# The forget gate of a two-block transformer kernel: logits with tokens on partitions instead of heads on partitions

## The chip, the cores and the metric

The kernel is one program on one core of a Trainium2 chip. The metric is the device time of one execution in microseconds. The kernel before the change takes 981.37 us (median of three runs, 980.94 to 981.79).

## The reference, cut to what matters

Two transformer blocks run on 256 tokens of width 1024 in float32. The first has a mixer (a gated convolution beside "forgetting attention" with eight heads) and a SwiGLU layer; the second has two SwiGLU layers, a hybrid mixer and an attention over a memory. The change touches the forget gate of the first block alone:

```python
f_logit = (h @ w_in)[..., 1536:1544]          # eight heads, 1024 inputs
logf = log_sigmoid(f_logit + b_f)             # [256 tokens, 8 heads]
c = cumsum(logf, axis=tokens)
logits = q @ k.T / 8 + c[query] - c[key]      # per head, then the causal mask and the softmax
```

Here h is x after its RMS norm. The kernel multiplies by the gain ahead of the product and by the inverse deviation of the token behind it.

## The kernel before, in words

**Tiling.** Activations stand transposed, features on partitions and the 256 tokens along the row, as eight tiles of 128 x 256 (act_hi, act_lo). To get float32 accuracy from fp32r matmuls, each weight and each activation is split in a high and a low part, and a product is three matmuls (`three`, L426 to L430): high by high, high by low, low by high. All weights come as 161 chunks of 1 MB through a ring of three stages. SyncE issues a chunk's DMA when VectorE has freed its place; ScalarE copies it to w_hi (`hi`), VectorE subtracts to w_lo (`lo`), and TensorE multiplies (`up`, `up_tok`, `down`). The order on each engine is written out by hand, and engines meet only at semaphores.

**The forget gate.** It lies in the first mixer, between the chunks of q and k (0 to 3) and those of v (4, 5), g_b (6, 7) and g_c (8, 9):

- SyncE loads the eight columns of w_in to wf (L381), and four copies of b_f into row 102 of par_rows, at columns 0, 32, 64 and 96 (L313).
- ScalarE and VectorE write wf four times over, 32 columns apart, into zeroed tiles wf_hi and wf_lo of 8 x 128 columns (L1128, L1694). GpSimd zeroes them at the start (L2131, L2132).
- TensorE transposes the parameter rows (L680) and then multiplies (L683): for each of eight k, `three` with the 128 columns of wf_hi or wf_lo stationary and 256 tokens moving, so 24 matmuls. The result stands in bank AUX with 128 partitions (four copies of eight heads, the rest zero) and 256 tokens along the row.
- VectorE scales by rs, adds the bias and forms -|z| (L1710 to L1713), ScalarE takes exp and ln (L1136, L1138), VectorE subtracts (L1717). All are 128 x 256 wide.
- TensorE turns the logarithm by two transposes (L695) after chunk 7, VectorE copies it to logf_tok (L1728), TensorE goes through chunk 8 and then sums it with the triangular matrix tri (L699 to L703), which gives c with tokens on partitions (c_tok, L1733) and with heads on partitions (negc, L1149). `aux` makes TensorE wait for the bank AUX. A_F, A_LOGF and A_CUM number its uses.

The names of the tiles: gate_banks in a row of the trace is the bank AUX in this stretch (it is the fourth half of that tensor), up_banks holds the results of `up`, mix_hi and mix_lo hold wf_hi and wf_lo, forget holds fz, fe and logf.

Of the kernel before, what the change touches and what calls it, by code (L numbers as in the profile page):

```python
# [14 lines left out]
F32 = mybir.dt.float32  # L15
F32R = mybir.dt.float32r
ALU = mybir.AluOpType
ACT = mybir.ActivationFunctionType
AX = mybir.AxisListType.X

P = 128
T = 256
D = 1024
KD = D // P
# [8 lines left out]
Q, K, V, GB, GC, HC, GATE_C, GATE_A = 0, 2, 4, 6, 8, 10, 12, 16  # L33
# [42 lines left out]
N_X0, N_MEM, N_POST0, N_FFN0, N_POST1, N_FFN1, N_MIX2, N_MEMQ, N_FFN2, N_OUT = range(10)  # L76
ROWS = [N_X0, N_FFN0, N_FFN1, N_MIX2, N_FFN2]


A_F, A_LOGF, A_CUM = 0, 1, 2  # L80
A_DQ = [3, 4]
A_DK = [5, 6]
A_BEFORE_FFN = [3, 3, 7]


G_MIX_PRE, G_MIX_POST, G_FFN_PRE, G_FFN_POST = 0, 8, 16, 24
G_FFN1, G_MIX2, G_MEMQ, G_MEMKV, G_FFN2 = 32, 40, 48, 56, 64
CONV, RETN, DIFN, MQN, MKN, DQN, DKN, LAMQ, LAMK, BF = 80, 92, 93, 94, 96, 98, 99, 100, 101, 102

C_ID, C_ONE, C_HALVES, C_TRI, C_CAUSAL, C_END = 0, 128, 256, 384, 640, 896  # L90

# [1 line left out]
def build(nc, a, out):  # L93
    with ExitStack() as ctx:
# [11 lines left out]
        act_hi, act_lo = act_both[:, :, 0, :], act_both[:, :, 1, :]  # L106
        mix_hi = sb("mix_hi", [P, KD, T], F32R)
        mix_lo = sb("mix_lo", [P, KD, T], F32R)
# [6 lines left out]
        rs = sb("rs", [P, T])  # L115
# [14 lines left out]
        par = sb("par", [P, P])  # L130
        first_rows = sb("first_rows", [KD, P])
        first_gain = sb("first_gain", [P, KD])
        wf = sb("wf", [P, KD, 8])
        forget = sb("forget", [P, 4, T])
        fz, fe, logf = (forget[:, i, :] for i in range(3))
        logf_tok = sb("logf_tok", [P, 2, P])
        c_tok = sb("c_tok", [P, 2, 8])
        small = sb("small", [P, 160])
# [7 lines left out]
        mem_T = q_pad[:, :, :, :].rearrange("p a b t -> p (a b) t")  # L146
        p_T0 = mem_T
        p_T1 = k_T[:, :, :].rearrange("p a b -> p (a b)").rearrange("p (m q) -> p m q", m=8)
        wf_hi = mix_hi[:, 0:4, :].rearrange("p a b -> p (a b)").rearrange("p (k n) -> p k n", k=KD)
        wf_lo = mix_lo[:, 0:4, :].rearrange("p a b -> p (a b)").rearrange("p (k n) -> p k n", k=KD)  # L150
        v_flat = v_mem[:, :, :].rearrange("p a b -> p (a b)")
        gb_T = v_flat[:, 0:1024].rearrange("p (a t) -> p a t", a=4)
        hc_T = v_flat[:, 1024:2048].rearrange("p (j a t) -> p j a t", j=2, a=2)
# [7 lines left out]
        sel_r = mix_hi[:, 4:8, :].rearrange("p a b -> p (a b)").rearrange("p (h m) -> p h m", h=8)  # L161
        negc = mix_lo[:, 4, :]
        q_T = q_pad[:, 0, :, :]
        wf_hi4, wf_lo4 = (w.rearrange("p k (g n) -> p k g n", g=4)[:, :, :, 0:8] for w in (wf_hi, wf_lo))
        wf4 = wf[:, :, None, :].to_broadcast([P, KD, 4, 8])
        alibi, decay = table[:, 0:4, :], table[:, 4:8, :]
        k_sq = [gate[:, 4 + 2 * t:6 + 2 * t, :].rearrange("p a b -> p (a b)") for t in range(2)]
        raw_dq = [gate[:, 8 + 2 * t:10 + 2 * t, :].rearrange("p a b -> p (a b)") for t in range(2)]
# [13 lines left out]
        ident = const[:, C_ID:C_ID + P]  # L182
# [7 lines left out]
        mean_sq, deviations, factors = ([norms[:, at + 2 * n:at + 2 * n + 2] for n in range(10)] for at in (40, 60, 80))  # L190
# [12 lines left out]
        bank = [x[:, i, :] for x in (up_banks, gate_banks) for i in range(2)]  # L203
# [3 lines left out]
        UP, SUM, AUX, ACC = 0, 2, 3, 4  # L207
# [84 lines left out]
        def parameters(engine):  # L292

            engine.wait_ge(zeroed, 3)

            def rows(r, n, src, cols=P, at=0):
                engine.dma_start(par_rows[r:r + n, at:at + cols], src).then_inc(par_landed, 16)

            for r, name in ((G_MIX_PRE, "norm_mix_pre"), (G_FFN_PRE, "norm_ffn_pre"), (G_FFN1, "norm_ffn1_2"), (G_MIX2, "norm_mix_2"),
                            (G_MEMQ, "norm_mem_q_2"), (G_MEMKV, "norm_mem_kv_2"), (G_FFN2, "norm_ffn2_2")):  # L300
                rows(r, KD, a[name][0].rearrange("(k p) -> k p", p=P))
            rows(CONV, 12, a["conv_w"][0].rearrange("j (b p) -> (j b) p", p=P))
            rows(RETN, 1, a["ret_norm_2"])
            rows(DIFN, 1, a["diff_norm_2"])
            rows(MQN, 2, a["mem_q_norm_2"][0].rearrange("(k p) -> k p", p=P))
            rows(MKN, 2, a["mem_k_norm_2"][0].rearrange("(k p) -> k p", p=P))
            for r, name in ((DQN, "diff_q_norm_2"), (DKN, "diff_k_norm_2")):
                rows(r, 1, a[name], 64, 0)
                rows(r, 1, a[name], 64, 64)
            for r, at, name in ((LAMQ, 0, "lambda_q1_2"), (LAMQ, 64, "lambda_q2_2"),  # L310
                                (LAMK, 0, "lambda_k1_2"), (LAMK, 64, "lambda_k2_2")):
                rows(r, 1, a[name], 64, at)
            for at in range(0, P, 32):  # L313
                rows(BF, 1, a["b_f"], 8, at)

        def store(engine, t, j):
            cols = slice(512 * j, 512 * j + 512)
# [107 lines left out]
        def _(pe):  # L425
            def three(dst, w, lo_w, x, lo_x, first, last, group=True):  # L426

                pe.matmul(dst, w, x, start=first, stop=False, skip_group_check=not group)  # L428
                pe.matmul(dst, w, lo_x, start=False, stop=False, skip_group_check=not group)  # L429
                return pe.matmul(dst, lo_w, x, start=False, stop=last, skip_group_check=not group)  # L430
# [38 lines left out]
            def up(c, hi, lo, ready=None, base=0, between=None):  # L469
                up_bank(c)  # L470
                up_product(pair[UP + BANK[c]], c % RING, hi, lo, ready, base, between=between)
# [46 lines left out]
            def aux(n):  # L518
                if n:
                    pe.wait_ge(aux_free, n)  # L520
# [154 lines left out]
            up(K, act_hi, act_lo)  # L675

            up(K + 1, act_hi, act_lo)
            pe.wait_ge(par_landed, 16 * 24)
            pe.wait_ge(rs_done, 1)
            pe.transpose(bank[SUM][:, 0:P], par_rows[:, :], ident).then_inc(par_turned, 1)  # L680
            pe.wait_ge(wf_lo_done, 1)
            aux(A_F)
            for k in range(KD):  # L683
                mm = three(bank[AUX][:, 0:T], wf_hi[:, k, :], wf_lo[:, k, :], act_hi[:, k, :], act_lo[:, k, :],
                           k == 0, k == KD - 1)
            mm.then_inc(aux_done, 1)
            tokens(V, act_hi, act_lo)
            pe.wait_ge(par_ready, 2)
            pe.matmul(bank[SUM][:, 0:2], ones, lam_p, start=True, stop=True).then_inc(lam_done, 1)
            up(GB, act_hi, act_lo)  # L690
            up(GB + 1, act_hi, act_lo)
            pe.wait_ge(logf_done, 1)
            aux(A_LOGF)
            for t in range(2):
                mm = pe.transpose(bank[AUX][:, t * P:t * P + P], logf[:, t * P:t * P + P], ident)  # L695
            mm.then_inc(aux_done, 1)
            up(GC, act_hi, act_lo)
            aux(A_CUM)
            pe.matmul(bank[AUX][:, 0:8], tri[:, 0:P], logf_tok[:, 0, 0:8], start=True, stop=True)  # L699
            pe.matmul(bank[AUX][:, 8:16], tri[:, P:T], logf_tok[:, 0, 0:8], start=True, stop=False)  # L700
# [73 lines left out]
            for j in range(4):  # L774
                pe.wait_ge(act_lo_done, 8 + 2 * j + 2)
                s = slice(2 * j, 2 * j + 2)
# [218 lines left out]
        def _(act):  # L995
# [128 lines left out]
            rows_out(N_X0, SUM)  # L1124
            hi(3)
            act.wait_ge(wf_landed, 16)
            act.wait_ge(zeroed, 6)
            act.activation(wf_hi4, wf4, copy).then_inc(wf_hi_done, 1)  # L1128
            hi(4)
            hi(5)  # L1130
            hi(6)
# [365 lines left out]
        def _(dve):  # L1497
            steps = [0]

            def then(ins):  # L1500

                steps[0] += 1
                ins.then_inc(dve_step, 1)
                dve.wait_ge(dve_step, steps[0])
# [182 lines left out]
                dve.scalar_tensor_tensor(q_T[:, b:b + 2, :], src, 0.125, over(rs), ALU.mult, ALU.mult).then_inc(up_free, 1)  # L1687

            query(Q)
            dve.wait_ge(zeroed, 6)  # L1690
            lo(3)
            query(Q + 1)
            dve.wait_ge(wf_hi_done, 1)
            dve.tensor_tensor(wf_lo4, wf4, wf_hi4.bitcast(F32), ALU.subtract).then_inc(wf_lo_done, 1)  # L1694

            lo(4)
            scaled(K, k_T[:, 0:2, :], rs)
# [9 lines left out]
            lo(6)  # L1707

            dve.wait_ge(aux_done, A_F + 1)
            dve.tensor_tensor(fz, bank[AUX][:, 0:T], rs[:, :], ALU.mult).then_inc(aux_free, 1)  # L1710
            dve.wait_ge(aux_free, A_F + 1)
            then(dve.tensor_scalar(fz, fz, par[:, BF:BF + 1], None, ALU.add))
            dve.scalar_tensor_tensor(fe, fz, -1.0, fz, ALU.mult, ALU.min).then_inc(fz_done, 1)  # L1713
            lo(7)
            lo(8)
            dve.wait_ge(fln_done, 1)
            dve.scalar_tensor_tensor(logf, fz, 0.0, fe, ALU.min, ALU.subtract).then_inc(logf_done, 1)  # L1717
            scaled(GB, gb_T[:, 0:2, :], rs)
            lo(9)
            scaled(GB + 1, gb_T[:, 2:4, :], rs)  # L1720
# [3 lines left out]

            then(dve.tensor_scalar(par[:, DIFN:DIFN + 1], par[:, DIFN:DIFN + 1], 1.0 - LAM_INIT, None, ALU.mult))
            lo(10)
            dve.wait_ge(aux_done, A_LOGF + 1)
            dve.tensor_copy(logf_tok[:, :, :].rearrange("p t q -> p (t q)"), bank[AUX][:, 0:2 * P]).then_inc(aux_free, 1)  # L1728
            scaled(GC, z_T[:, 0:2, 2:T + 2], rs)
            lo(11)  # L1730
            dve.wait_ge(aux_done, A_CUM + 1)
# [387 lines left out]
        @block.gpsimd  # L2119
        def _(pool):  # L2120
            steps = [0]

            def then(ins):
                steps[0] += 1
                ins.then_inc(pool_step, 1)
                pool.wait_ge(pool_step, steps[0])

            pool.memset(small[:, :], 0.0).then_inc(zeroed, 1)
            pool.memset(eps_t[:, :], EPS).then_inc(zeroed, 1)
            pool.memset(par_rows[:, :], 0.0).then_inc(zeroed, 1)  # L2130
            pool.memset(wf_hi.bitcast(F32), 0.0).then_inc(zeroed, 1)  # L2131
            pool.memset(wf_lo.bitcast(F32), 0.0).then_inc(zeroed, 1)  # L2132
            pool.memset(z_T[:, :, 0:2], 0.0).then_inc(zeroed, 1)
            for j in range(2):
                wait_read(pool, HC + j)
                zs = z_T[:, 2 * j:2 * j + 2, 2:T + 2]
                pool.tensor_tensor(zs, zs, hc_T[:, j, :, :], ALU.mult).then_inc(z_done, 1)
            pool.wait_ge(kf_done, 1)
            for h in range(4):
                wait_read(pool, MEMK + h - h % 2 + 1)  # L2140
                for t in range(2):
                    k = raw_k[:, t, 256 * h:256 * h + 256]
                    ins = pool.tensor_scalar(k, k, k_f[:, 2 * h + t:2 * h + t + 1], None, ALU.mult)
                ins.then_inc(kscaled_done, 1)
# [37 lines left out]
```

## Time and profile before

| What | Before |
|---|---|
| Time, median of three runs | 981.37 us |
| Time of the profiled execution | 981.42 us |
| Its span, first to last instruction | 979.6 us |
| Mean granted TensorE clock | 0.998 |
| TensorE busy with matmuls | 969.3 us (99%), 5588 matmuls |
| VectorE busy | 678.3 us (69%) |
| ScalarE busy | 495.5 us (51%) |
| Share of TensorE in the chain that ended last | 94% |

The profiled execution took 1.8 us more than its span, and 0.05 us more than the median of the three runs. The page's busy times say how full an engine is; the chain that ended last says which of them set the end. A group of rows names the line of the kernel, the engine, the operation and the tiles, written before read. The recorded length of a matmul contains its way through the array and overlaps the next one, so the pace of a run of matmuls is read from the chain, whose pieces don't overlap. A matmul on plain float32 operands appears as two instructions (x2); an fp32r matmul and a transpose appear as one.

### The profile page before, as it was taken

The numbers are of one execution on the slowest core, as the hardware profiler recorded it, in microseconds if no ns is written. First come the engines' busy times: TensorE is split into PE (matmuls) and PEld (weight loads), VectorE is DVE, ScalarE is ACT, GpSimd is POOL, SyncE is SP. The second block draws the span as 40 slices with busy tenths as digits, with TensorE's granted clock in tenths as the row PEclk, the third lists the DMA queues.
The fourth block names the chain that finished last, engine by engine and source line by source line (L and its number), as shares of the span: only waits on it lengthen the run. The fifth ranks groups of instructions, "written<-read, shape, count | busy, mean of one in ns | idle before, by whom it ended". The sixth has DMA issues, their size and how long they took to land.

```text
span 979.6 us, 14008 instructions
## 1 busy us (share of the span) xinstructions
PE 969.3 (99%) x5588; PEld 851.5 (87%) x5588; DVE 678.3 (69%) x697; ACT 495.5 (51%) x666; POOL 16.7 (2%) x20
## 2 busy tenths in 40 slices
PE   9999999999999999999999999999999999999997
PEld 8999999888888888888888888899888888888885
DVE  5557867757777677877776776675664577777776
ACT  6354565773343434834434346574856554343433
POOL 0000000022000000000000000000000000000000
PEclk9999999999999999999999999999999999999999
DMA  7855474654555556555555563635444445656551
GB/s 237 279 175 171 129 280 130 229 181 140 204 192 198 187 193 214 172 163 197 189 184 188 194 214 129 215 130 172 156 146 151 154 148 172 214 171 214 171 171 43
DMA packets 122309, 176.23 MB, mean 180 GB/s; under 512 B 4042, under 2 KB 94364, under 8 KB 122140
## 3 DMA queue, kind: packets, MB, share of 16 engines
q1 hardware_dynamic: 121548, 173.23, 53.3%
q10 hardware_dynamic: 720, 2.43, 0.7%
q8 instruction: 29, 0.48, 0.2%
q14 instruction: 12, 0.10, 0.0%
HBM read 174.60 MB, written 1.05 MB: 179 GB/s over the span
## 4 chain that ended last, share of the span: by engine, by line
PE 94%; DVE 2%; ACT 1%; DMA 1%; issue 1%; SPq 0%; DVEq 0%; ACTq 0%
PE up_banks L581 12%; PE gate_banks L581 12%; PE bank L428 9%; PE bank L429 9%; PE bank L430 9%; PE up_banks L428 9%; PE up_banks L430 8%; PE up_banks L429 8%; PE up_banks L586 6%; PE gate_banks L586 6%; DMA stage<-in_w_in 1%; PE bank L515 1%; DVE w_lo L1513 1%; PE bank L532 1%; PE bank L723 0%
## 5 line engine op out<-in xcount | busy, mean ns | idle before, releaser
L1519 DVE TENSOR_TENSOR w_lo<-stage,w_hi 128x2048 fp32r<-128x2048 f32 x81 | 185.5, 2290 | 96.6 <-ACT w_hi L1011 96.6
L1513 DVE TENSOR_TENSOR w_lo<-stage,w_hi 128x2048 fp32r<-128x2048 f32 x79 | 180.8, 2293 | 83.9 <-ACT w_hi L1004 83.7
L1004 ACT ACTIVATE w_hi<-stage 128x2048 fp32r<-128x2048 f32 x79 | 150.8, 1911 | 72.9 <-PE up_banks L430 36.0
L1011 ACT ACTIVATE w_hi<-stage 128x2048 fp32r<-128x2048 f32 x81 | 152.8, 1904 | 0.0
L581 PE MATMUL gate_banks<-act_both,w_hi 128*128 128x512 f32 x528 | 135.5, 393 | 0.5 <-DVE act_both L1526 0.5
L581 PE MATMUL up_banks<-act_both,w_hi 128*128 128x512 f32 x528 | 131.7, 391 | 0.0
L581 PEld LDWEIGHTS up_banks<-act_both,w_hi 128*128 128x128 f32 x528 | 96.6, 188 | 18.4
L581 PEld LDWEIGHTS gate_banks<-act_both,w_hi 128*128 128x128 f32 x528 | 93.8, 189 | 16.5 <-DVE act_both L1526 0.7
L428 PE MATMUL up_banks<-act_both,w_hi 128*128 128x256 f32 x352 | 100.9, 287 | 0.9 <-DVE w_lo L1513 0.5
L429 PE MATMUL up_banks<-act_both,w_hi 128*128 128x256 f32 x352 | 99.5, 283 | 0.0
L430 PE MATMUL up_banks<-act_both,w_lo 128*128 128x256 f32 x352 | 99.5, 283 | 0.0
L1086 ACT ACTIVATE ffn_hi<-gate 128x512 fp32r<-128x512 f32 x30 | 18.9, 632 | 155.7 <-DVE gate L1635 155.7
L428 PE MATMUL bank<-w_hi,ffn_hi 128*128 128x512 f32 x240 | 94.0, 392 | 0.2 <-DVE ffn_lo L1637 0.2
L429 PE MATMUL bank<-w_lo,ffn_hi 128*128 128x512 f32 x240 | 93.7, 390 | 0.0
L430 PE MATMUL bank<-w_hi,ffn_lo 128*128 128x512 f32 x240 | 93.4, 389 | 0.0
L1079 ACT ACTIVATE gate<-gate 128x512 f32<-128x512 f32 x33 | 20.9, 632 | 129.9 <-DVE gate L1623 129.9
L586 PEld LDWEIGHTS gate_banks<-act_both,w_lo 128*128 128x128 f32 x528 | 74.5, 190 | 6.8
L586 PEld LDWEIGHTS up_banks<-act_both,w_lo 128*128 128x128 f32 x528 | 72.0, 190 | 5.1
L586 PE MATMUL gate_banks<-act_both,w_lo 128*128 128x256 f32 x528 | 76.4, 282 | 0.0
L586 PE MATMUL up_banks<-act_both,w_lo 128*128 128x256 f32 x528 | 73.6, 282 | 0.0
L428 PEld LDWEIGHTS up_banks<-act_both,w_hi 128*128 128x128 f32 x352 | 67.4, 192 | 2.4 <-issue 2.0
L429 PEld LDWEIGHTS up_banks<-act_both,w_hi 128*128 128x128 f32 x352 | 67.5, 192 | 0.0
(339 smaller groups left out, 1535.7 us busy)
## 6 DMA issues: line engine op xcount, KB each, us to landing
stage<-in_ffn_w SPq DMA_DIRECT2D x66, 1024.0 KB, 5.3
stage<-in_w_in SPq DMA_DIRECT2D x33, 1024.0 KB, 5.3
stage<-in_w_gate_up SPq DMA_DIRECT2D x22, 1024.0 KB, 5.1
stage<-in_w_down SPq DMA_DIRECT2D x11, 1024.0 KB, 4.9
stage<-in_w_out SPq DMA_DIRECT2D x8, 1024.0 KB, 4.9
stage<-in_mem_w_kv SPq DMA_DIRECT2D x8, 1024.0 KB, 5.1
stage<-in_w_branch SPq DMA_DIRECT2D x4, 1024.0 KB, 5.2
stage<-in_mem_w_q SPq DMA_DIRECT2D x4, 1024.0 KB, 5.0
```

The lines of the kernel that those rows point to most:

```text
L428: pe.matmul(dst, w, x, start=first, stop=False, skip_group_check=not group)
L429: pe.matmul(dst, w, lo_x, start=False, stop=False, skip_group_check=not group)
L430: return pe.matmul(dst, lo_w, x, start=False, stop=last, skip_group_check=not group)
L515: mm = pe.transpose(pair[ACC + p][:, m, t * P:t * P + P], x_n[:, t, d0:d0 + P], ident)
L581: return pe.matmul(banks[:, m, :], wh[:, k, m * P:m * P + P], act_both[:, k, :, :].rearrange("p s t -> p (s t)"), start=k == 0, stop=False ...
L586: return pe.matmul(banks[:, m, T:2 * T], wl[:, k, m * P:m * P + P], act_both[:, k, 0, :], start=False, stop=k == KD - 1, skip_group_check= ...
L1004: act.activation(w_hi[:, place, :], stage[:, place, :], copy).then_inc(hi_done, 1)
L1011: act.activation(w_hi[:, place, :], stage[:, place, :], copy).then_inc(hi_done, 1)
L1079: act.activation(silu, g_s, ACT.Silu).then_inc(silu_done, 1)
L1086: act.activation(to, h_T, copy).then_inc(ffn_hi_done, 1)
L1513: dve.tensor_tensor(w_lo[:, place, :], stage[:, place, :], w_hi[:, place, :].bitcast(F32), ALU.subtract).then_inc(lo_done, 1)
L1519: dve.tensor_tensor(w_lo[:, place, :], stage[:, place, :], w_hi[:, place, :].bitcast(F32), ALU.subtract).then_inc(lo_done, 1)
```

## The change

The operands of the gate's product change sides. The activations become the stationary side (128 tokens of one k-tile) and the gate's weights the moving side. One tile wf_both holds for each k sixteen columns, eight of the high part and eight of the low. For each of two groups of 128 tokens and each k there are two matmuls: act_hi by all sixteen columns, and act_lo by the first eight, added onto the second eight of the result. That is 32 matmuls. The result has tokens on partitions. One tensor_reduce adds the two halves, and all functions work on 16 numbers a partition (2 groups x 8 heads). The scale of a token is now a number of its partition, and the bias is loaded once, broadcast to 128 partitions, into a part of forget. The last subtraction writes logf_tok directly, four copies 32 columns apart, in a tile that GpSimd zeroes. The transposes of the logarithm, their copy and the use A_LOGF of the bank are gone, and TensorE's wait for logf_done moves from ahead of chunk 8 to behind it. The two memsets of wf_hi and wf_lo give way to one of logf_tok.

```diff
-A_F, A_LOGF, A_CUM = 0, 1, 2
+A_F, A_CUM = 0, 1
...
-        fz, fe, logf = (forget[:, i, :] for i in range(3))
+        fz, fe, neg = (forget[:, i, 0:16].rearrange("p (t n) -> p t n", t=2) for i in range(3))
+        b_f = forget[:, 3, 0:8]
...
-            for at in range(0, P, 32):
-                rows(BF, 1, a["b_f"], 8, at)
+            engine.dma_start(b_f[:, :], a["b_f"][0:1, :].to_broadcast([P, 8])).then_inc(par_landed, 16)
...
-            pe.wait_ge(par_landed, 16 * 24)
+            pe.wait_ge(par_landed, 16 * 21)
             pe.wait_ge(rs_done, 1)
             pe.transpose(bank[SUM][:, 0:P], par_rows[:, :], ident).then_inc(par_turned, 1)
             pe.wait_ge(wf_lo_done, 1)
             aux(A_F)
-            for k in range(KD):
-                mm = three(bank[AUX][:, 0:T], wf_hi[:, k, :], wf_lo[:, k, :], act_hi[:, k, :], act_lo[:, k, :],
-                           k == 0, k == KD - 1)
+            for t in range(2):
+                ts = slice(t * P, t * P + P)
+                for k in range(KD):
+                    pe.matmul(bank[AUX][:, 16 * t:16 * t + 16], act_hi[:, k, ts], wf_both[:, k, :], start=k == 0 and t == 0, stop=False,
+                              skip_group_check=True)
+                    mm = pe.matmul(bank[AUX][:, 16 * t + 8:16 * t + 16], act_lo[:, k, ts], wf_both[:, k, 0:8], start=False,
+                                   stop=k == KD - 1, skip_group_check=True)
             mm.then_inc(aux_done, 1)
...
             up(GB + 1, act_hi, act_lo)
+            up(GC, act_hi, act_lo)
             pe.wait_ge(logf_done, 1)
-            aux(A_LOGF)
-            for t in range(2):
-                mm = pe.transpose(bank[AUX][:, t * P:t * P + P], logf[:, t * P:t * P + P], ident)
-            mm.then_inc(aux_done, 1)
-            up(GC, act_hi, act_lo)
             aux(A_CUM)
...
-            act.wait_ge(zeroed, 6)
-            act.activation(wf_hi4, wf4, copy).then_inc(wf_hi_done, 1)
+            act.activation(wf_both[:, :, 0:8], wf[:, :, :], copy).then_inc(wf_hi_done, 1)
...
-            dve.tensor_tensor(wf_lo4, wf4, wf_hi4.bitcast(F32), ALU.subtract).then_inc(wf_lo_done, 1)
+            dve.tensor_tensor(wf_both[:, :, 8:16], wf[:, :, :], wf_both[:, :, 0:8].bitcast(F32), ALU.subtract).then_inc(wf_lo_done, 1)
...
             dve.wait_ge(aux_done, A_F + 1)
-            dve.tensor_tensor(fz, bank[AUX][:, 0:T], rs[:, :], ALU.mult).then_inc(aux_free, 1)
+            halves_sum = bank[AUX][:, 0:32].rearrange("p (t s n) -> p t n s", t=2, s=2)
+            dve.tensor_reduce(fz, halves_sum, AX, ALU.add).then_inc(aux_free, 1)
             dve.wait_ge(aux_free, A_F + 1)
-            then(dve.tensor_scalar(fz, fz, par[:, BF:BF + 1], None, ALU.add))
+            dve.wait_ge(r_done, N_X0 + 1)
+            for t in range(2):
+                ins = dve.scalar_tensor_tensor(fz[:, t, :], fz[:, t, :], factors[N_X0][:, t:t + 1], b_f, ALU.mult, ALU.add)
+            then(ins)
+            then(dve.tensor_scalar(neg, fz, 0.0, None, ALU.min))
             dve.scalar_tensor_tensor(fe, fz, -1.0, fz, ALU.mult, ALU.min).then_inc(fz_done, 1)
             lo(7)
             lo(8)
             dve.wait_ge(fln_done, 1)
-            dve.scalar_tensor_tensor(logf, fz, 0.0, fe, ALU.min, ALU.subtract).then_inc(logf_done, 1)
+            dve.wait_ge(zeroed, 4)
+            dve.tensor_tensor(logf4, neg[:, :, None, :].to_broadcast([P, 2, 4, 8]), fe[:, :, None, :].to_broadcast([P, 2, 4, 8]),
+                              ALU.subtract).then_inc(logf_done, 1)
...
             lo(10)
-            dve.wait_ge(aux_done, A_LOGF + 1)
-            dve.tensor_copy(logf_tok[:, :, :].rearrange("p t q -> p (t q)"), bank[AUX][:, 0:2 * P]).then_inc(aux_free, 1)
             scaled(GC, z_T[:, 0:2, 2:T + 2], rs)
...
-            pool.memset(wf_hi.bitcast(F32), 0.0).then_inc(zeroed, 1)
-            pool.memset(wf_lo.bitcast(F32), 0.0).then_inc(zeroed, 1)
+            pool.memset(logf_tok[:, :, :], 0.0).then_inc(zeroed, 1)
```

## Rows read from the trace of the kernel before

**Rows 1.** The page: busy time by engine; the chain's shares by engine.

```profile
PE 969.3 (99%) x5588; PEld 851.5 (87%) x5588; DVE 678.3 (69%) x697; ACT 495.5 (51%) x666; POOL 16.7 (2%) x20
...
PE 94%; DVE 2%; ACT 1%; DMA 1%; issue 1%; SPq 0%; DVEq 0%; ACTq 0%
```

**Rows 2.** Windows: start:end length, busy (instructions) of PE, PEld, DVE, ACT, POOL, clock, DMA.

```profile
36.00:39.00 3.00, 3.00 (x27) 2.96 (x26) 2.83 (x3) 0.18 (x2) 0.00 (x0) 1.00 1.10 349
```

**Rows 3.** The chain, 34 to 40 us: start, length on the chain, what.

```profile
35.91 0.11 PE gate_banks L680
36.02 0.12 PE gate_banks L428
...
38.90 0.23 PE up_banks L428
```

**Rows 4.** The chain from 61 to 61.9 us, around the transposes of the logarithm.

```profile
61.55 0.22 PE gate_banks L695 x2
```

**Rows 5.** The chain from 67.1 to 69 us, the sums with tri.

```profile
67.64 0.22 PE gate_banks L700 x2
67.86 0.22 PE gate_banks L701 x2
68.09 0.53 PE gate_banks L702 x2
```

**Rows 6.** Groups by form, weight loads: busy us, mean ns of one | idle before.

```profile
L429 PEld LDWEIGHTS gate_banks<-act_both,mix_hi 128*128 128x128 f32 x8 | 1.5, 191 | 0.0
...
L700 PEld LDWEIGHTS gate_banks<-logf_tok,const 128*128 128x128 f32 x2 | 0.3, 192 | 0.0
...
L695 PEld LDWEIGHTS gate_banks<-const,forget 128*128 128x128 f32 x2 | 0.2, 140 | 0.0
...
L743 PEld LDWEIGHTS bank<-k_T,v_tok 128*64 128x64 f32 x16 | 1.1, 137 | 0.6
```

**Rows 7.** Timeline of TensorE: start, length, line and operation.

```profile
35.76 0.27 PE L680 MATMUL gate_banks<-const,par_rows 128*128 128x128 f32 x1
35.78 0.37 PE L428 MATMUL gate_banks<-act_both,mix_hi 128*128 128x256 f32 x1
```

**Rows 8.** Timeline of VectorE, 36 to 72 us.

```profile
36.17 2.29 DVE L1513 TENSOR_TENSOR w_lo<-stage,w_hi 128x2048 fp32r<-128x2048 f32 x1 [1.76 <-ACT w_hi L1004]
...
43.11 0.42 DVE L1710 TENSOR_TENSOR forget<-gate_banks,rs 128x256 f32<-128x256 f32 x1
...
43.95 0.43 DVE L1713 SCALAR_TENSOR_TENSOR forget<-forget 128x256 f32<-128x256 f32 x1
...
55.37 0.42 DVE L1717 SCALAR_TENSOR_TENSOR forget<-forget 128x256 f32<-128x256 f32 x1
...
71.77 0.17 DVE L1733 COPY c_tok<-gate_banks 128x16 f32<-128x16 f32 x1
```

**Rows 9.** Timeline of ScalarE: the copy of chunk 4's weights to w_hi.

```profile
29.56 1.92 ACT L1004 ACTIVATE w_hi<-stage 128x2048 fp32r<-128x2048 f32 x1 [5.52 <-DMA stage<-in_w_in]
```

**Rows 10.** Timeline of SyncE's issues around the bias.

```profile
23.31 1.14 SPq L297 DMA_DIRECT2D par_rows<-in_b_f  x4
24.49 0.94 SPq L342 DMA_DIRECT2D stage<-in_w_in  x2
```

**Rows 11.** Timeline of TensorE, the first 10 us.

```profile
1.05 4.64 PE L650 MATMUL gate_banks<-L 128*128 128x128 f32 x20 [1.05 <-DVE L L1663]
...
5.82 1.51 PE L661 MATMUL bank<-const,x_n 128*128 128x128 f32 x8
7.16 2.84 PE L664 MATMUL gate_banks<-L 128*128 128x128 f32 x24
```

**Rows 12.** Windows at the end, columns as in rows 2.

```profile
972.00:974.00 2.00, 0.35 (x2) 0.00 (x0) 1.90 (x4) 1.22 (x4) 0.00 (x0) 1.00 0.00 0
974.00:976.00 2.00, 0.00 (x0) 0.00 (x0) 1.08 (x4) 1.63 (x3) 0.00 (x0) 1.00 0.02 6
976.00:978.00 2.00, 0.00 (x0) 0.00 (x0) 0.00 (x0) 0.00 (x0) 0.00 (x0) 0.53 0.98 376
```

More of the change, by code:

```diff
@@ L77 @@
 ROWS = [N_X0, N_FFN0, N_FFN1, N_MIX2, N_FFN2]
-A_F, A_LOGF, A_CUM = 0, 1, 2
-A_DQ = [3, 4]
-A_DK = [5, 6]
-A_BEFORE_FFN = [3, 3, 7]
+A_F, A_CUM = 0, 1
+A_DQ = [2, 3]
+A_DK = [4, 5]
+A_BEFORE_FFN = [2, 2, 6]
 G_MIX_PRE, G_MIX_POST, G_FFN_PRE, G_FFN_POST = 0, 8, 16, 24
 G_FFN1, G_MIX2, G_MEMQ, G_MEMKV, G_FFN2 = 32, 40, 48, 56, 64
-CONV, RETN, DIFN, MQN, MKN, DQN, DKN, LAMQ, LAMK, BF = 80, 92, 93, 94, 96, 98, 99, 100, 101, 102
+CONV, RETN, DIFN, MQN, MKN, DQN, DKN, LAMQ, LAMK = 80, 92, 93, 94, 96, 98, 99, 100, 101
 C_ID, C_ONE, C_HALVES, C_TRI, C_CAUSAL, C_END = 0, 128, 256, 384, 640, 896
@@ L148, in build @@
         p_T1 = k_T[:, :, :].rearrange("p a b -> p (a b)").rearrange("p (m q) -> p m q", m=8)
-        wf_hi = mix_hi[:, 0:4, :].rearrange("p a b -> p (a b)").rearrange("p (k n) -> p k n", k=KD)
-        wf_lo = mix_lo[:, 0:4, :].rearrange("p a b -> p (a b)").rearrange("p (k n) -> p k n", k=KD)
+        wf_both = mix_hi[:, 0, 0:P].rearrange("p (k n) -> p k n", k=KD)
         v_flat = v_mem[:, :, :].rearrange("p a b -> p (a b)")
@@ L163, in build @@
         q_T = q_pad[:, 0, :, :]
-        wf_hi4, wf_lo4 = (w.rearrange("p k (g n) -> p k g n", g=4)[:, :, :, 0:8] for w in (wf_hi, wf_lo))
-        wf4 = wf[:, :, None, :].to_broadcast([P, KD, 4, 8])
+        logf4 = logf_tok[:, :, :].rearrange("p t (g n) -> p t g n", g=4)[:, :, :, 0:8]
         alibi, decay = table[:, 0:4, :], table[:, 4:8, :]
@@ L1689, in _ @@
             query(Q)
-            dve.wait_ge(zeroed, 6)
+            dve.wait_ge(zeroed, 5)
             lo(3)
```

## The prediction

> **What bounds the kernel now.** I read the page first. TensorE is busy for 969.3 of 979.6 us, and 94% of the chain that ended last is TensorE's own matmuls, one behind another [rows 1]. So a change counts by what it does to TensorE's stream, and work taken from the other engines counts only where TensorE waits for them. Then I read the stretch of the gate in windows: TensorE is busy for all of it, at the full granted clock [rows 2]. Last I read the chain in that stretch, since the recorded lengths overlap and only the chain gives the pace. The chain goes L680, then the gate's 24 matmuls, then the first matmul of chunk 4, with no piece of another engine between [rows 3]. The same holds for the transposes of the logarithm [rows 4] and for the sums with tri [rows 5].
>
> **Part 1: the product changes sides.** Removed: 24 matmuls with 256 moving columns. They hold the chain from 36.02 to 38.90 us [rows 3], which is 2.88 us, or 0.12 us each. Added: 32 matmuls with 16 or 8 moving columns, each with a fresh load of 128 stationary columns. The number of moving columns falls by a factor of sixteen, but the number of loads rises by a third, so the question is what a load costs when almost nothing moves behind it. The trace of before has matmuls with 8 moving columns: L700 and L701, four instructions that hold the chain from 67.64 to 68.09 us [rows 5], 0.45 us or 0.1125 us each. They are plain float32, and the new ones are fp32r. I take their pace for two reasons. First, the recorded load of 128 columns takes 191 ns for the gate's fp32r operands and 192 ns for L700's float32; the load of a transpose takes 140 ns [rows 6]. So an fp32r load behaves like the float32 one, not like the transpose's. Second, a load of 64 columns takes 137 ns [rows 6]: 64 columns more cost 55 ns, 128 columns cost 0.11 us, which is the pace of L700 and L701. L701 also adds onto the bank columns that L700 has just written (8 to 16) without a longer step, so that adding onto the same few columns costs nothing. The sum: 32 x 0.1125 = 3.60 us, against 2.88 us, is +0.72 us.
>
> The bounds of this term: no better than 0.12 us each, the pace that fp32r has now, gives 3.84 us and +0.96 us. On the other side, if loads were as quick as a transpose's, 52 ns shorter than 192 ns [rows 6], the pace would be 0.06 us: 1.92 us, and -0.96 us. The closest two starts of matmuls in the trace are L680 at 35.76 and L428 at 35.78 us [rows 7], with the second load done beforehand. By that pace, some 0.03 us, the product would take 0.96 us, and -1.92 us. That is the far end, the value if loads cost nothing.
>
> The Trainium skill has a rule that speaks for this far end: its page "TensorE: Matmul & The Clock Gate", section "Back-to-back issue gap", gives a gap of some 60 cycles (25 ns) for 1 to 64 moving columns, and the section before the steps says that start to start never falls under about 25 ns. By that alone the product would take 0.8 us as an estimate. The same section gives 81 ns for a sustained pair of load and matmul with 128 columns moving, by which it would take 2.6 us. Neither figure says which operand type it is for; the rows of L700 and L701 (0.1125 us) are above both, and the sum goes by them.
>
> **Part 2: no transposes of the logarithm.** The two transposes hold the chain for 0.22 us [rows 4]. They go, and chunk 8 follows chunk 7 directly: -0.22 us. Their copy on VectorE (L1728) ended before TensorE needed it, so it costs nothing now and saves nothing. TensorE's wait for logf_done moves from ahead of chunk 8 to behind it. logf is written at 55.37 to 55.79 us [rows 8], and TensorE comes to its new place at about 67.5 us, so this wait has over 11 us of slack. Queued behind it would be the sums and the logits; nothing waits there.
>
> **Part 3: VectorE and ScalarE.** Three operations that run from 43.11 to 44.38 us, 1.27 us in all (L1710 to L1713, [rows 8]), give way to five on 8 to 32 columns. The nearest row is the copy of 16 columns out of PSUM, 0.17 us [rows 8]; five of these are 0.85 us, plus their waits on each other. That is some 0.3 us less. L1717 falls from 0.42 us to between 0.17 and 0.42 us, and L1694 and L1128 likewise; exp and ln on ScalarE get shorter too. All of it is cover, worth 0 on the chain: v's second chunk is split by 38.46 us [rows 8] and used some 5 us later. The functions come after the product; if that ends 0.7 us later, VectorE still reaches it only at 43.11 us [rows 8], over 3 us after its end at about 39.6 us. The new waits (r_done, zeroed at 4) are for things finished in the first 20 us. On GpSimd two memsets give way to a smaller one, at a time when nobody waits for it.
>
> **Part 4: the bias.** SyncE issues four tiny DMAs now, 1.14 us in all [rows 10]; it will issue one with 128 rows of 32 bytes. A load of 128 rows costs 0.47 us to issue (half of 0.94 us [rows 10]). So chunk 4's load is issued about 0.7 us earlier. ScalarE waits for that chunk at 29.56 us [rows 9], and a gain there only adds to slack that TensorE doesn't use. The new DMA stands ahead of chunk 4 in the same queue and should have landed when that chunk has, at 29.56 us, 6 us before TensorE's wait for par_landed at 35.7 us. If this cover were gone, TensorE would stand there for the difference. I cost it at 0.
>
> **The sum.** +0.72 - 0.22 = +0.50 us. The profiled execution took 981.42 us, 0.05 us over the median, so the forecast is 981.42 + 0.50 = 981.9 us. With the pace of 0.12 us it is +0.74, or 982.2 us. The measurement itself moved by 0.4 us either way around the median. Within 0.2% (1.96 us), which is about what a measurement of this kernel can tell from no change, this is the same time.
>
> **Rival 1: the clock falls (slower).** Now TensorE streams 256 columns in every 0.12 us. In the new product it streams 12 on average in every 0.11 us, for 3.6 us on end: the instructions follow each other, but the array is nearly empty. The granted clock follows what the engine does: it was still 1.00 in the window 974 to 976 us, and at the low level (1.2 GHz) for nearly all of 976 to 978, when TensorE had done nothing since 972.35 us [rows 12]. That is a fall after some 3.7 us of idleness. If the thin product counts as idle, the clock can fall near its end, and chunk 4 starts at the low level. The place is the stream from 38.9 us on; from there the loss is half of the time spent low. The start of the kernel shows such a time: from 1.05 us the steps are 0.22 us each (20 in 4.64 us), and they come down during L661, so that the 24 steps of L664 from 7.16 us take 0.12 us each [rows 11]. That is some 5.5 us, of which half, 2.7 us, is lost: 981.9 + 2.7 = 984.6 us. If the fall comes late or the return sooner, half of it: 983.3 us. It decides from the point at which thin matmuls no longer count as work. For it: the share of the array in use, 5%. Against it: the load port is busy throughout, and no stretch of the trace of before falls in clock; but no stretch is as thin for as long, so the trace can't exclude it. The Trainium skill, page "TensorE: Matmul & The Clock Gate", section "What's actually happening", says that the gate goes by how busy the engine has been recently, and doesn't say whether thin matmuls count. Chance 0.20.
>
> **Rival 2: loads are hidden (faster).** The product runs at the pace of short matmuls, 0.03 us, and the change is -1.92 - 0.22 = -2.1 us: 979.3 us. At the transpose's load it is -0.96 - 0.22 = -1.2 us: 980.2 us. For it: nothing moves to speak of, and the page cited above. Against it: 0.1125 us at 8 columns [rows 5], and the load times [rows 6]. Chance 0.08 for both, 0.04 for a time near 979.3.
>
> **Rival 3: the bias lands late (slower).** 128 small rows join a busy queue. If they landed a whole chunk later than I think, with chunk 5, at about 34 us, TensorE would still not wait. It takes over 6 us of delay to cost the first microsecond. Chance 0.02, at 983 us.
>
> **How the numbers follow.** The sum has the other 0.70, at 981.5 to 982.4 us with the bounds of its pace and the runs' own spread. The range leaves out the lower half of rival 2 and the upper half of rival 1: 980.9 to 984.0 us. Slower by over 0.2% is over 983.3 us: most of rival 1, 0.16, and a little for surprises, 0.17. Faster by over 0.2% is under 979.4 us: 0.04. Same: 0.79.
>
> **What would show it.** In the chain of the changed kernel, 32 pieces of some 0.11 us from the first gate matmul to chunk 4, against 24 of 0.12 us now; pieces of 0.03 or 0.06 us would make part 1 wrong. No L695, and chunk 8's first piece 0.12 us after chunk 7's last. The granted clock in windows from 36 to 50 us: 1.00 for the sum, under 1.00 with steps of some 0.45 us in chunk 4 for rival 1. VectorE's five operations at some 0.17 us. No idle time ahead of L680; a wait there would be rival 3. TensorE's matmuls: 5588 + 8 - 2 = 5594.

## The result, and the profile after

The changed kernel takes 983.62 us (median of eleven executions, 981.72 to 985.44) against 981.46 us (980.89 to 981.79): a ratio of 1.0023, with a 95% interval of 1.0016 to 1.0031. The forecast was 981.9 us, 1.7 us less. The kernel is slower by 2.2 us, and its times are spread over 3.7 us where those of before are spread over 0.9 us. The profiled execution took 985.1 us with a span of 983.2 us, 3.6 us more than the span of before.

The page of the changed kernel, the same lines as in [rows 1], and the clock's line of section 2 (40 slices, tenths of full speed):

```profile
PE 972.9 (99%) x5594; PEld 854.7 (87%) x5594; DVE 677.6 (69%) x698; ACT 494.8 (50%) x666; POOL 15.2 (2%) x19
...
PEclk9899999999999999999999999999999999999999
...
PE 95%; DVE 3%; ACT 1%; issue 1%; DVEq 0%; ACTq 0%
```

TensorE is again busy all the time; it has 3.6 us more of it, for six more matmuls. One digit is an 8: the second slice, 24.6 to 49.2 us, where the gate lies. The windows of that stretch in the changed kernel (columns as in [rows 2], which shows 1.00):

```profile
36.00:38.00 2.00, 2.00 (x20) 2.00 (x20) 1.00 (x4) 0.18 (x1) 0.00 (x0) 0.99 1.10 348
38.00:40.00 2.00, 2.00 (x11) 2.00 (x11) 0.24 (x1) 1.73 (x1) 0.00 (x0) 0.50 1.11 349
40.00:42.00 2.00, 2.00 (x5) 1.55 (x6) 2.00 (x2) 0.00 (x0) 0.00 (x0) 0.50 0.90 284
...
44.00:46.00 2.00, 2.00 (x8) 1.61 (x8) 0.00 (x0) 0.00 (x0) 0.00 (x0) 0.80 1.03 362
46.00:48.00 2.00, 2.00 (x10) 1.65 (x10) 0.00 (x0) 0.11 (x1) 0.00 (x0) 1.00 0.30 101
```

TensorE is "busy" for every microsecond of it. The granted clock, the last column but two, falls to 0.50 (1.2 GHz) at 38.0 us and is back at 1.00 (2.4 GHz) before 45 us. The chain of the changed kernel in this stretch (start, length on the chain, what), which answers to [rows 3]; L684 and L686 are the new matmuls, L678 the transpose of the parameter rows, L426 to L428 chunk 4:

```profile
35.46 0.11 PE gate_banks L678
35.57 0.01 PE gate_banks L684
35.58 0.11 PE gate_banks L686
35.69 0.12 PE gate_banks L684
...
37.92 0.12 PE gate_banks L684
38.03 0.15 PE gate_banks L686
38.19 0.22 PE gate_banks L684
...
39.69 0.21 PE gate_banks L686
39.89 0.63 PE up_banks L426
40.53 0.43 PE up_banks L427
...
44.79 0.28 PE up_banks L428
45.08 0.23 PE up_banks L426
```

The reader is to see three paces. From 35.58 to 38.03 us, 22 of the new matmuls take 0.111 us each. After the clock has fallen, eight more take 0.21 us each. Then come twelve steps of chunk 4, which took 0.23 us each before: the first takes 0.63 us, ten take 0.43 us, and the last, in which the clock comes back, takes 0.28 us. The account: the product holds the chain for 39.89 - 35.57 = 4.32 us against 2.88 us, +1.44; the twelve steps of chunk 4 take 5.19 us against 12 x 0.2275 = 2.73 us, +2.46; the transposes of the logarithm are gone, -0.22. That is +3.7 us. The sums with tri begin 3.22 us later than before, at 70.74 instead of 67.52 us, in an execution in which the gate began 0.45 us sooner (L678 at 35.46 instead of 35.91). So all of the loss lies between 35 and 45 us.

VectorE's work at the gate in the changed kernel (timeline), to hold against [rows 8], and SyncE's issue of the bias against [rows 10]:

```profile
41.97 0.18 DVE L1708 TENSOR_REDUCE forget<-gate_banks 128x16 f32<-128x32 f32 x1
42.19 0.36 DVE L1712 SCALAR_TENSOR_TENSOR forget<-forget,norms 128x8 f32<-128x8 f32 x2
42.59 0.17 DVE L1714 TENSOR_SCALAR forget<-forget 128x16 f32<-128x16 f32 x1
42.80 0.17 DVE L1715 SCALAR_TENSOR_TENSOR forget<-forget 128x16 f32<-128x16 f32 x1
...
58.40 0.22 DVE L1720 TENSOR_TENSOR logf_tok<-forget 128x64 f32<-128x64 f32 x1
```

```profile
22.19 0.36 SPq L312 DMA_DIRECT2D forget<-in_b_f  x1
22.59 0.98 SPq L340 DMA_DIRECT2D stage<-in_w_in  x2
```

### The profile page after: what moved, and what is told of

The parts are those of the page before. It is cut to its first block, busy times and chain, and to the rows that moved or that the text cites. A ratio compares the mean times of both kernels' runs of the same rounds, so it can differ in the third digit from the quotient of the medians.

```text
span 983.2 us, 14018 instructions
## 1 busy us (share of the span) xinstructions
PE 972.9 (99%) x5594; PEld 854.7 (87%) x5594; DVE 677.6 (69%) x698; ACT 494.8 (50%) x666; POOL 15.2 (2%) x19
## 4 chain that ended last, share of the span: by engine, by line
PE 95%; DVE 3%; ACT 1%; issue 1%; DVEq 0%; ACTq 0%
PE up_banks L579 12%; PE gate_banks L579 12%; PE bank L426 9%; PE bank L427 9%; PE bank L428 9%; PE up_banks L426 9%; PE up_banks L428 9%; PE up_banks L427 9%; PE up_banks L584 6%; PE gate_banks L584 6%; PE bank L513 1%; PE bank L530 1%; PE gate_banks L648 0%; DVE w_lo L1510 0%; PE bank L721 0%
## 5 line engine op out<-in xcount | busy, mean ns | idle before, releaser
L426 PE MATMUL up_banks<-act_both,w_hi 128*128 128x256 f32 x352 | 100.7, 286 | 0.6 <-DVE w_lo L1665 0.6
L428 PE MATMUL up_banks<-act_both,w_lo 128*128 128x256 f32 x352 | 99.5, 283 | 0.0
L426 PE MATMUL bank<-w_hi,ffn_hi 128*128 128x512 f32 x240 | 94.0, 392 | 0.2 <-DVE ffn_lo L1634 0.2
L428 PE MATMUL bank<-w_hi,ffn_lo 128*128 128x512 f32 x240 | 93.4, 389 | 0.0
L426 PEld LDWEIGHTS up_banks<-act_both,w_hi 128*128 128x128 f32 x352 | 67.4, 192 | 1.8 <-issue 1.6
```

## The experiments

The theory after the result, called the clock theory: a block made only of thin matmuls (few moving columns) makes the granted clock fall, as idleness does, and the loss is what is multiplied at 1.2 GHz until the clock is back. Its rivals: the thin matmuls cost what they cost wherever they stand; the loads or the exchanged operands, not the few columns, bring the clock down; something else in this place of the kernel does. All runs below are compared with the kernel before on the same chip, 981.55 us for e1 to e4, 981.56 us for e5 to e8 and 981.62 us for e9 (medians). There is a limit to this: e1 to e4 ran on one chip and e5 to e9 on another. The changed kernel ran again (e7) on the second alone, and which chip gave its first times is not on record. So it isn't shown that the clock falls in the changed kernel on the chip of e1 to e3, whose 33 executions all stayed under 982.6 us. What the second chip shows by itself is e7 and e8 (it falls), e9 (it doesn't), and the pair e5 and e6.

### The same work, spread: e1_spread

```diff
             for m in range(2):
                 for k in range(KD):
                     mm = three(dst[:, m, :], wh[:, k, m * P:m * P + P], wl[:, k, m * P:m * P + P],
                                act_hi[:, k, :], act_lo[:, k, :], k == 0, k == KD - 1)
+                    if k % 2:
+                        gate_pair(0, 4 * m + k // 2)
...
+                    gm = gate_pair(1, 4 * t + k)
```

gate_pair(t, k) issues the two thin matmuls of token group t and k-tile k.

> The changed kernel with its 32 thin matmuls in sixteen pairs, eight between the groups of chunk 3 and eight between those of the first half of chunk 4, instead of in one block. Clock theory (the block of thin matmuls makes the granted clock fall): the same work without the block, so the granted clock stays at 1.00 from 30 to 60 us and only the pace is left, 32 x 0.1125 - 2.88 - 0.22 = +0.5 us on before, about 981.9 us, all runs within 0.5 us of each other. Rival (the time is lost by what the thin matmuls are, by their bank writes or their loads, and not by standing together): no better than the changed kernel, +2 us on before, and again three levels of time.

Measured: 982.15 us (981.62 to 982.55, eleven executions), 0.6 us more than before; ratio 1.0005 (0.9996 to 1.0014). Its windows, columns as above:

```profile
36.00:38.00 2.00, 2.00 (x18) 1.91 (x17) 1.51 (x3) 0.00 (x0) 0.00 (x0) 1.00 1.11 349
38.00:40.00 2.00, 2.00 (x12) 1.72 (x11) 0.58 (x4) 1.40 (x1) 0.00 (x0) 1.00 1.10 348
40.00:42.00 2.00, 2.00 (x14) 1.72 (x12) 1.45 (x1) 0.52 (x1) 0.00 (x0) 1.00 1.10 349
```

The clock stays at 1.00, and the spread of the times is that of before. The same 32 matmuls cost 1.5 us less in the median when they don't stand together, which speaks against the rival that lays the loss on them one by one (if the changed kernel loses its 2 us on this chip too).

### Two blocks of half the length: e2_two_blocks

```diff
+            pe.wait_ge(wf_lo_done, 1)
+            aux(A_F)
+            for k in range(KD):
+                gate_pair(0, k)
             up(K + 1, act_hi, act_lo)
...
+            for k in range(KD):
+                gm = gate_pair(1, k)
```

> The changed kernel with its 32 thin matmuls in two blocks of sixteen (1.8 us each) with the whole of chunk 3 between them. Clock theory: what counts is how long TensorE is thin on end; half the length makes the fall rarer or absent, between +0.5 us (981.9) and +1.5 us. Rival (each thin stretch costs something whatever its length, at its start or end): as the changed kernel or worse, +2 us or more on before.

Measured: 981.88 us (981.63 to 982.54, eleven executions), +0.3 us on before; ratio 1.0004 (0.9995 to 1.0013). No execution reached the changed kernel's middle level, and all windows of the profile from 30 to 60 us stand at 1.00. Blocks of sixteen (1.8 us) with a chunk between them did no harm on this chip. The rival that each thin stretch lowers the clock, whatever its length, finds no support.

### Wider and as many: e3_wide128 and e8_wide32

```diff
-        wf_both = mix_hi[:, 0, 0:P].rearrange("p (k n) -> p k n", k=KD)
+        wf_both = mix_hi[:, 0:4, :].rearrange("p a b -> p (a b)")[:, 0:128 * KD].rearrange("p (k n) -> p k n", k=KD)
...
+                    pe.matmul(bank[AUX][:, at:at + 128], act_hi[:, k, ts], wf_both[:, k, :], ...)
+                    mm = pe.matmul(bank[AUX][:, at + 8:at + 128], act_lo[:, k, ts], wf_both[:, k, 0:128 - 8], ...)
```

e8_wide32 has 32 in every place of 128.

> The changed kernel with 128 and 120 moving columns in place of 16 and 8 (copies of the gate's weights fill the rest and their results aren't used). The block, its loads and its place stay. Clock theory in the form that columns count and loads don't: the pace stays at that of the load, about 0.11 us, so the block still takes 3.6 us, and the clock stays at 1.00: +0.5 us on before, about 981.9 us. Rival (the loads at this pace, or the switch of operands, make the clock fall): low clock as in the changed kernel, +2 us or more. If 128 columns cost more than the load, the pace rises to 0.12 us and it is +0.7 us.

Measured: 981.95 us (981.43 to 982.32, eleven executions), +0.4 us on before; ratio 1.0003 (0.9994 to 1.0012). Its chain, and its windows:

```profile
36.09 0.11 PE gate_banks L687
...
39.44 0.11 PE gate_banks L687
39.55 0.29 PE up_banks L426
```

```profile
38.00:40.00 2.00, 2.00 (x17) 1.92 (x17) 1.51 (x5) 1.02 (x1) 0.00 (x0) 1.00 1.11 331
40.00:42.00 2.00, 2.00 (x11) 1.63 (x10) 1.07 (x1) 0.89 (x1) 0.00 (x0) 1.00 1.03 332
```

Number, loads, place and length of the block are the changed kernel's: it ends at 39.55 us, 3.5 us after it began, with 0.11 us for each matmul. So 128 moving columns cost no more than 16: they pass while the next load runs. In TensorE's stream only the columns differ (ScalarE makes one more copy to fill them), and the clock doesn't fall in eleven executions. So on this chip neither the loads nor the exchanged sides bring it down.

> The changed kernel with 32 and 24 moving columns, twice to three times the changed kernel's and a quarter of e3_wide128's, at the same pace of 0.11 us. Clock theory in the form that columns count: the array is still all but empty (28 columns take 0.012 us of 0.1125), so the clock still falls, +1.5 to +2 us on before. Rival (only the emptiest matmuls, of 8 and 16, are not seen as work): 981.9 us and the clock at 1.00.

Measured: 983.73 us (982.02 to 985.82, nine executions); ratio 1.0025 (1.0015 to 1.0035). The three levels of the changed kernel are back: one execution at 982.0, five from 983.4 to 983.9, three from 985.2 to 985.8 us. The windows of its profile:

```profile
38.00:40.00 2.00, 2.00 (x17) 2.00 (x17) 0.31 (x2) 0.96 (x1) 0.00 (x0) 0.87 1.10 348
40.00:41.00 1.00, 1.00 (x3) 0.81 (x4) 0.01 (x1) 0.95 (x1) 0.00 (x0) 0.50 1.10 350
...
43.00:44.00 1.00, 1.00 (x6) 0.82 (x5) 0.92 (x5) 0.00 (x0) 0.00 (x0) 1.00 0.17 57
```

By this pair, with the same block and the same pace, the number of moving columns decides; but its two halves ran on different chips, and the pair that has one chip is e5 and e6 below. Where between 32 and 128 columns it turns was not measured. The rival that the clock falls only behind the emptiest matmuls, of 8 and 16 columns, is out.

### The block alone, in the kernel before: e5_before_thin and e6_before_thick

```diff
             up(GB, act_hi, act_lo)
+            aux(A_LOGF)
+            for t in range(2):
+                for k in range(KD):
+                    for part in (act_hi, act_lo):
+                        pe.matmul(bank[AUX][:, T:T + 16], part[:, k, t * P:t * P + P], wf_hi[:, 0, 0:16],
+                                  start=True, stop=True, skip_group_check=True)
             up(GB + 1, act_hi, act_lo)
```

e6_before_thick writes T:T + 256 and moves act_hi[:, 0, :], 256 columns.

> The kernel before, whole, with 32 matmuls of 16 moving columns added in one block between chunks 6 and 7, written to unused columns of the bank and read by nobody. Clock theory: their own time is 32 x 0.1125 = 3.6 us, and the block makes the clock fall here too, though nothing of the change is in the kernel: +3.6 us where it doesn't fall, +5.4 and +7.2 us where it does for one or two stretches (the steps between the changed kernel's levels are 1.8 us), so about 987 us with levels that far apart. Rival (the low clock comes from something in the changed kernel around chunk 3 and 4, the DMAs or the state at 38 us): +3.6 us, 985.1 us, in every run and the clock at 1.00 in the block.

> The same kernel as e5_before_thin with 256 moving columns in each of the 32 added matmuls instead of 16. Both theories: 32 x 0.12 = 3.84 us, 985.3 us, in every run, and the clock at 1.00. What the thin block costs beyond its pace is e5 less this run, plus 0.24 us: under the clock theory 1.5 to 2 us in the median, under its rival 0.

Measured: e5 takes 987.93 us (986.62 to 988.21, five executions), e6 985.38 us (985.0 to 985.65, five executions); the ratios to before are 1.0065 (1.0052 to 1.0079) and 1.0039 (1.0026 to 1.0053). The chains of e5 (first fence) and e6 (second), and e5's windows (third):

```profile
55.87 3.47 PE gate_banks L695 x32
59.35 0.22 PE up_banks L428
...
60.04 0.12 PE up_banks L430
60.16 0.19 PE up_banks L428
...
60.57 0.21 PE up_banks L430
```

```profile
55.46 3.84 PE gate_banks L695 x32
59.30 0.12 PE up_banks L428
```

```profile
59.00:60.00 1.00, 1.00 (x11) 1.00 (x11) 1.00 (x1) 0.00 (x0) 0.00 (x0) 1.00 1.05 371
60.00:62.00 2.00, 2.00 (x12) 2.00 (x11) 0.34 (x1) 0.00 (x0) 0.00 (x0) 0.52 0.29 38
62.00:64.00 2.00, 2.00 (x13) 2.00 (x12) 0.00 (x0) 0.00 (x0) 0.00 (x0) 0.63 0.99 336
64.00:66.00 2.00, 2.00 (x19) 2.00 (x18) 0.00 (x0) 0.00 (x0) 0.00 (x0) 1.00 0.49 167
```

The thin block with the first step behind it is 0.27 us shorter than the thick one with its own (3.47 + 0.22 against 3.84 + 0.12), and the kernel takes 2.55 us more: 2.8 us are lost to the low clock in the median, more than the 1.5 to 2 us that I had expected. The reason is that four of the five executions lie at the upper level (987.9 to 988.2 us, mean clock 0.995) and one, the profiled one, at the lower (986.62 us, 0.997); none lies at e6's level. The low clock of this profile lasts 3.4 us (60.1 to 63.5), in which a step takes 0.21 instead of 0.12 us, so it costs 1.5 us, and twice as long costs 3.0 us. In e6 the windows from 50 to 70 us stand at 1.00.

In this profile of e5 the clock is still at 1.00 when the block ends, at 59.35 us, and falls some 0.7 us later, six steps into chunk 7. It is not the matmuls that are running when it falls that bring it down, but those that came before. The place is 20 us later, and no other part of the change is in the kernel, so the rival that something else in the changed kernel does it is out. With one chip, one place, as many loads and all five executions on either side, this pair is the firmest evidence that few moving columns make the clock fall. (The thick block also moves another tile, act_hi in place of wf_hi; no run parts that from the number of columns, but e8, which moves the changed kernel's weights, falls as well.)

### The changed kernel again: e7_after_again

> The changed kernel once more. Clock theory: the three levels of its first eleven times come back, at about 981.8, 983.5 and 985.3 us, the fall being a matter of how the block lies to something that runs free of the kernel; median +2 us on before. Rival (the levels were the chip's or the hour's): one level.

Measured: 983.78 us (981.89 to 985.35, eleven executions); ratio 1.0024 (1.0015 to 1.0033). Of all 22 executions of the changed kernel, two lie at 981.7 to 981.9 us with a mean clock of 0.998 as before, fourteen from 983.0 to 984.0 us with 0.996 or 0.997, six from 984.8 to 985.4 us with 0.995. Two of the 22 were profiled; for the others the length of the low clock is inferred from the time and the mean clock. The windows of this profile, from the middle level:

```profile
38.00:40.00 2.00, 2.00 (x12) 1.89 (x12) 0.96 (x4) 1.60 (x1) 0.00 (x0) 0.70 1.04 301
...
41.00:42.00 1.00, 1.00 (x4) 0.81 (x3) 1.00 (x1) 0.00 (x0) 0.00 (x0) 0.50 1.08 379
42.00:43.00 1.00, 1.00 (x5) 0.77 (x5) 0.96 (x4) 0.00 (x0) 0.00 (x0) 0.90 0.56 191
```

Here the clock is low for about 3.4 us (from 38.8 to 42.2 us); in the profile at the top level, 985.1 us, it was low for 6.8 us. A step takes 0.43 instead of 0.2275 us at the low level, and a thin matmul 0.21 instead of 0.11 us, so somewhat under half of that time is lost: some 1.6 and 3.2 us. The middle and the top level lie about 1.7 and 3.4 us above the lowest.

### The sides the other way round: e4_narrow and e9_narrow_again

```diff
+            for k in range(KD):
+                mm = pe.matmul(bank[AUX][0:16, :], wf_both[:, k, :], act_both[:, k, :, :].rearrange("p s t -> p (s t)"),
+                               start=k == 0, stop=k == KD - 1)
+            mm.then_inc(aux_done, 1)
+            up_tok(V, act_hi, act_lo, 0)
+            aux(A_Z)
+            for t in range(2):
+                mm = pe.matmul(bank[AUX][:, 8 * t:8 * t + 8], z_rows[:, t * P:t * P + P], add_up[:, :], start=True, stop=True)
+            mm.then_inc(aux_done, 1)
+            up_tok(V, act_hi, act_lo, 1)
...
+            then(dve.tensor_tensor(add_up[:, :], ident[0:16, 0:8], ident[0:16, 8:16], ALU.add))
+            dve.wait_ge(aux_done, A_F + 1)
+            dve.tensor_reduce(z_rows[:, :], bank[AUX][0:16, :].rearrange("p (s t) -> p t s", s=2), AX, ALU.add).then_inc(aux_free, 1)
```

> The other way round: the sixteen columns [high | low] are the stationary side and act_both with its 512 columns moves, so the product is 8 matmuls instead of 32 and gives 16 partitions by 512. VectorE adds high and low activations (one tensor_reduce), and a float32 matmul of each 128 tokens with a 16 x 8 matrix adds high and low weights and puts the tokens on partitions; the functions on eight columns stay. By the rows: 8 x 0.2275 = 1.82 us, plus four instructions of 0.1125 us = 0.45 us, against 2.88 + 0.22 us of before: -0.8 us, about 980.6 us, with the clock at 1.00 since nothing is thin for long. Against the changed kernel with its low clock -2.9 us. Rival (the time around the gate isn't TensorE's but that of the chain through VectorE): the float32 matmuls wait for VectorE's sum and it is no better than before, 981.4 us.

> e4_narrow once more, since 0.6 us is near what a measurement can tell. From the chain of e4_narrow: the product takes 1.85 us, the float32 matmuls 0.54 us and the step behind them 0.43 us in place of 0.23 us, so 1.85 + 0.54 + 0.20 - 2.88 - 0.22 = -0.5 us on before: 981.0 us, at a clock of 1.00 from 30 to 60 us, if the gain is real. Rival (its 0.6 us was chance): within 0.2 us of before.

Measured: 980.94 us (980.52 to 981.27) against 981.55 us, and again 981.00 us (980.26 to 981.49) against 981.62 us, eleven executions each. Both ratios are 0.9994, with intervals of 0.9984 to 1.0003 and 0.9985 to 1.0003. Its chain in e4:

```profile
35.62 1.85 PE gate_banks L684 x8
37.47 0.24 PE up_banks L428
...
42.98 0.54 PE gate_banks L690 x4
43.52 0.43 PE up_banks L428
```

Eight matmuls of 512 columns take 1.85 us, where 1.82 was worked out. The small float32 matmuls take 0.54 us instead of 0.45, and the step behind them 0.43 us instead of 0.23, which I had left out: -0.5 instead of -0.8 us. A longer step behind thin matmuls is not peculiar to float32. In e1 it stands behind each thin fp32r pair:

```profile
35.46 0.01 PE gate_banks L677
35.47 0.11 PE gate_banks L679
35.58 0.23 PE up_banks L426
```

There the step of 0.12 us takes 0.11 us more, and the first thin matmul takes 0.01 us. So the pair still costs 0.23 us in all, two times 0.11. In e4 nothing is given back in this way, and why is open.

The clock stays at 1.00 from 30 to 60 us. This version is 2.7 us faster than the changed kernel (e9 against e7, on one chip: 2.8 us). Against the kernel before it is 0.6 us faster twice over, but each interval still takes in 1, so that gain is likely and not proved.

## Why the prediction was right or wrong, point by point

**The number and the range.** 983.62 us lies in the range of 980.9 to 984.0 us, but not where the likeliest case put it. What came true is rival 1, with a chance of 0.20. Its price, 983.3 to 984.6 us, holds the median; its place (the stream behind the product) and its kind (low clock, steps of 0.43 us in chunk 4) are what the trace shows. The forecast of 981.9 us itself was met only by the executions without a fall, 2 of 22. The failed step is the weighing of that rival: the sum took the clock to stay at 1.00 through the thin product, with a chance of 0.70. I held against it that the load port is busy throughout and that no stretch of the trace before falls in clock. The runs show that busy loads don't hold the clock up: e5 and e6 have the same 32 loads of 128 columns each, and the clock falls in e5 and not in e6. And the trace of before had no stretch of the kind, so its silence was no evidence. There was luck in the size. The rival's low time of 5.5 us was read off the start of the kernel, by its paces alone (the windows from 0 to 6 us print a granted clock of 1.00 all the same, though the trace's record of it has its first entry at 6.7 us), and halved without a row that says so. What was measured is 3.4 or 6.8 us, falling at 38.0 us in one profile and 38.8 us in the other, in the last third of the product, about where the rival had it. The upper end of the range, 984.0 us, leaves out the top level, on which six of the 22 executions lie.

**Part 1, the pace: right.** 0.1125 us was taken from four float32 matmuls with 8 columns [rows 5]; the new fp32r ones take 0.111 us. The longer load [rows 6] decided, not the columns. Where the clock doesn't fall, the whole change costs +0.3 us (981.7 and 981.9 us, two executions), and its spread and wider versions +0.3 to +0.6 us, for a forecast of +0.50 us.

**Rival 2, hidden loads: wrong.** The first of the block takes 0.01 us on the chain, like the start of L428 close behind L680 in [rows 7]; the other 31 do not follow it. The Trainium skill's page "TensorE: Matmul & The Clock Gate", section "Back-to-back issue gap", has some 25 ns for 1 to 64 moving columns and 81 ns for a pair of load and matmul with 128; the trace doesn't agree with either for fp32r with a load for each matmul, 0.111 us. The section "LDWEIGHTS (loading the stationary operand)" of the same page of the Trainium skill divides the number of columns by 1.2 GHz, as an estimate 107 ns for 128. The pace of 111 ns at the full clock agrees with that within 5%; the 0.21 us at the low clock doesn't.

**The clock.** The granted clock fell in a stretch in which the engine's record was 100% busy, as it does after idleness [rows 12], and in e5 it fell 0.7 us after the thin block had ended. The section "What's actually happening" of the same page of the Trainium skill has the gate follow how busy the engine has been recently. e5 agrees as to "recently"; that thin matmuls can go uncounted, that page of the Trainium skill doesn't say.

**Part 2: right in kind.** The transposes are gone from the chain, and nothing waits at the new place: logf_tok was written by 58.62 us, and the sums began at 70.74 us. The 0.22 us itself was not run alone.

**Parts 3 and 4: right, worth nothing on the chain.** VectorE's operations take 1.00 us (41.97 to 42.97) instead of 1.27. The bias costs SyncE 0.36 us instead of 1.14; I had written 0.47. No idle time appears ahead of L678, so rival 3 is out in this trace.

**What would show it.** The list named low clock from 36 to 50 us with steps of some 0.45 us in chunk 4 as the sign of rival 1, and 5594 matmuls. Both are there; the steps are 0.43 us, and the clock was low from 38.0 to 44.8 us in the one profile and from 38.8 to 42.2 us in the other.

## What to carry to other kernels

When the sides of a matmul are exchanged to move fewer columns, count the loads: with a fresh load of 128 fp32r columns for each, the matmul costs the load, 0.11 us, from 8 moving columns up to 128. A small product is cheaper with its few columns stationary and the many moving (8 matmuls in 1.85 us here, or 2.6 us with the small ones that add up its parts, against 24 in 2.88 and 32 in 3.6 us). And look at the granted clock behind a block of thin matmuls: a busy share of 100% says nothing of how full the array is, and what follows the block may run at half the clock. Here a block of 3.6 us had such a fall in most executions. Spread between wide matmuls, or cut in two, the same matmuls had none in eleven executions each, though on another chip than the one on which the changed kernel was run again.

## What the runs showed of the hardware that was not expected

- The clock's fall varies by execution: 2 of 22 executions of one and the same program had none, fourteen lost some 1.7 us and six some 3.4 us. Times that lie on levels, with a mean clock that goes along (0.998, 0.997, 0.995), were the sign of such a stretch here.
- The fall can come after the stretch that causes it: 0.7 us behind the block in e5, six steps into a chunk of wide matmuls. The rows that run slow are then not the ones to mend.
- An fp32r load of 128 columns hides as many as 128 moving columns: 0.11 us a matmul with 16 and with 128.
- At the low clock, a thin matmul takes 0.21 us instead of 0.11, so the load that sets its pace slows down as well, and one with 512 columns takes 0.43 instead of 0.23 us.
- Thin matmuls make the step behind them longer: by 0.10 to 0.11 us behind the fp32r ones of e1 and e5, by 0.20 us behind the four float32 ones of e4 and e9. A sum that counts the thin matmuls alone misses this where, as in e4, nothing is given back at their start.
